# Gate and up tiles of a feed-forward phase interleaved on TensorE, with four slots of split weights

## The reference

```
x = x + mixed @ w_out                                   # 1024 -> 1024
h = rmsnorm(x, norm_ffn)
gate, ffn_new = causal_dwconv(h @ w_gate, ffn_past, ffn_conv_w, ffn_conv_b)   # width 3
x = x + (silu(gate) * (h @ w_up)) @ w_down              # 1024 -> 2816 -> 1024
```

## Time and profile before

| | us |
|---|---|
| three runs | 2597.19, 2600.63, 2600.97 |
| median | 2600.63 |
| the profiled execution | 2597.43 |
| its span in the trace | 2595.4 |

### The profile page before, as it was taken

The page is one execution under the profiler, slowest core; times in us unless marked ns, Lnnn a source line. Parts: engine busy times, 40 slices in busy tenths (PEclk is TensorE's granted clock), DMA queues, the critical chain, the costliest instruction groups (busy, mean ns, idle before and its releaser), DMA issues.

```text
span 2595.4 us, 33146 instructions
## 1 busy us (share of the span) xinstructions
PE 2368.6 (91%) x12571; PEld 2155.4 (83%) x12571; DVE 1057.6 (41%) x1983; ACT 999.4 (39%) x1676; POOL 1207.8 (47%) x629
## 2 busy tenths in 40 slices
PE   6999815977785799999999999999999999999998
PEld 6999814544443799999999999999999999999998
DVE  3687766059936433224332233231243231242212
ACT  4555311345552343344433334332333332343333
POOL 3544483025410455555455545444444444555554
PEclk9999958999996899999999999999999999999999
DMA  5544400200025454444543335433345333344443
GB/s 141 142 134 122 89 4 1 4 14 0 0 26 181 117 146 130 122 119 147 158 122 106 116 98 171 134 102 106 106 122 161 111 103 108 108 128 134 130 122 106
DMA packets 533462, 272.03 MB, mean 105 GB/s; under 512 B 95116, under 2 KB 527045, under 8 KB 533317
## 3 DMA queue, kind: packets, MB, share of 16 engines
q1 hardware_dynamic: 533317, 270.06, 36.7%
HBM read 252.65 MB, written 17.43 MB: 104 GB/s over the span
## 4 chain that ended last, share of the span: by engine, by line
PE 67%; DVE 1%; DMA 0%; SPq 0%; ACT 0%; issue 0%; ACTq 0%
PE ffn_bank L138 22%; PE ffn_bank L139 22%; PE ffn_bank L140 22%; PE ffn_bank L2323 1%; PE ffn_bank L2227 1%; DMA ffn_w_raw<-in_w_out 0%; DVE ffn_xm_lo L2060 0%; PE ffn_bank L2248 0%; SPq L1835 0%; DVE ffn_xT L2072 0%; DVE ffn_bank L2093 0%; DVE ffn_yrow L2143 0%; ACT ffn_xm_hi L1949 0%; SPq L1832 0%; SPq L1864 0%
## 5 line engine op out<-in xcount | busy, mean ns | idle before, releaser
L1928 POOL TENSOR_TENSOR ffn_w_lo<-ffn_w_raw,ffn_w_hi 128x1024 fp32r<-128x1024 f32 (+1 forms) x380 | 889.1, 2341 | 865.8 <-ACT ffn_w_hi L1937 865.6
L138 PE MATMUL ffn_bank<-ffn_xf_hi,ffn_w_hi 128*128 128x386 f32 (+5 forms) x1760 | 626.1, 356 | 5.7 <-DVE ffn_xf_lo L2124 5.7
L139 PE MATMUL ffn_bank<-ffn_xf_lo,ffn_w_hi 128*128 128x386 f32 (+5 forms) x1760 | 623.3, 354 | 0.0
L140 PE MATMUL ffn_bank<-ffn_xf_hi,ffn_w_lo 128*128 128x386 f32 (+5 forms) x1760 | 622.1, 353 | 0.0
L1937 ACT ACTIVATE ffn_w_hi<-ffn_w_raw 128x1024 fp32r<-128x1024 f32 (+1 forms) x380 | 391.5, 1033 | 579.4 <-PE ffn_bank L140 358.4
L138 PEld LDWEIGHTS ffn_bank<-ffn_xf_hi,ffn_w_hi 128*128 128x128 f32 x1760 | 331.9, 189 | 20.8 <-issue 6.3
L139 PEld LDWEIGHTS ffn_bank<-ffn_xf_lo,ffn_w_hi 128*128 128x128 f32 x1760 | 333.0, 189 | 12.3
L140 PEld LDWEIGHTS ffn_bank<-ffn_xf_hi,ffn_w_lo 128*128 128x128 f32 x1760 | 332.5, 189 | 12.1
L138 PE MATMUL ffn_bank<-ffn_h_hi,ffn_w_hi 128*128 128x384 f32 (+2 forms) x880 | 312.0, 355 | 3.6 <-DVE ffn_xT L2072 3.6
L140 PE MATMUL ffn_bank<-ffn_h_hi,ffn_w_lo 128*128 128x384 f32 (+2 forms) x880 | 310.1, 352 | 0.0
L139 PE MATMUL ffn_bank<-ffn_h_lo,ffn_w_hi 128*128 128x384 f32 (+2 forms) x880 | 309.7, 352 | 0.0
(11 more groups left out here) (350 smaller groups left out, 3178.7 us busy)
## 6 DMA issues: line engine op xcount, KB each, us to landing
ffn_w_raw<-in_w_gate SPq DMA_DIRECT2D x220, 256.0 KB, 3.3
ffn_w_raw<-in_w_up SPq DMA_DIRECT2D x220, 256.0 KB, 3.2
ffn_w_raw<-in_w_down SPq DMA_DIRECT2D x160, 256.0 KB, 3.1
pin_w_raw<-in_w_in SPq DMA_DIRECT2D x120, 256.0 KB, 3.4
ffn_w_raw<-in_w_out SPq DMA_DIRECT2D x160, 128.0 KB, 2.8
ffn_w_raw<-in_w_down SPq DMA_DIRECT2D x80, 192.0 KB, 2.6
mixed<-z_t SPq DMA_DIRECT2D x40, 208.0 KB, 2.2
pin_xrow<-in_x_prompt SPq DMA_DIRECT2D x15, 512.0 KB, 5.9
```

What stands on the lines that cost most here:

```text
L138: pe.matmul(out, w_hi, x_hi, start=first, stop=False)
L139: pe.matmul(out, w_hi, x_lo, start=False, stop=False)
L140: return pe.matmul(out, w_lo, x_hi, start=False, stop=last)
L1928: pool.tensor_tensor(w_lo[n % 3][:, 0:c], w_raw[n % 2][:, 0:c], w_hi[n % 3][:, 0:c].bitcast(F32), ALU.subtract).then_inc(s_lo, 1)
```

## The change

The gate and the up tile of a feature are computed together. For each of the eight slices, and each of the three passes, a matmul of the gate tile is followed by the matmul of the up tile with the same pass; they go to the two banks in turn. Both units must be split before the pair starts, so PE waits once, at the start of the pair, for `w_lo` of both, and for both of the things that a bank must be free of (`conv` for the gate bank, `h_lo` for the up bank). Both units are given back at the end of the pair. `w_hi` and `w_lo` get a fourth slot each, and ACT's `hi` runs four units ahead in place of three. The norm stages through two banks (2 and 3) in place of three, with `scaled_lo` of slice k-2 ahead of `scaled` of slice k on DVE. At the start of the phase the fourth `hi` is placed ahead of the fourth `mixed_hi`.

```diff
-        w_hi = [m.sb(f"w_hi{i}", [P, KD * P], F32R) for i in range(3)]
-        w_lo = [m.sb(f"w_lo{i}", [P, KD * P], F32R) for i in range(3)]
+        w_hi = [m.sb(f"w_hi{i}", [P, KD * P], F32R) for i in range(4)]
+        w_lo = [m.sb(f"w_lo{i}", [P, KD * P], F32R) for i in range(4)]
...
-        stage_b = bank[1:4]
+        stage_b = bank[2:4]
...
             def hi(n):
-                if n >= 3:
-                    act.wait_ge(s_used, n - 2)
+                if n >= 4:
+                    act.wait_ge(s_used, n - 3)
...
             def after(n):
 
-                if n + 3 < UNITS:
-                    hi(n + 3)
+                if n + 4 < UNITS:
+                    hi(n + 4)
...
-            for n in range(3):
+            for n in range(4):
                 hi(n)
                 mixed_hi(0, n)
-            mixed_hi(0, 3)
...
                     for k in hook.get(o, ()):
+                        if k >= 2:
+                            scaled_lo(b, k - 2)
                         scaled(b, k)
-                        if k:
-                            scaled_lo(b, k - 1)
                     if o == 5:
+                        scaled_lo(b, KD - 2)
                         scaled_lo(b, KD - 1)
...
             def gate_up(b, f):
-                fi, fw = b * NF + f, fwidth(b)
-                for s, (bk, c0) in enumerate(((gate_b[f % 2], 0), (up_b[f % 2], HALO))):
-                    n = n_gu(b, f, s)
-                    nb = HALO + fw - c0
-                    if fi >= 2:
-                        pe.wait_ge((s_conv, s_hlo)[s], fi - 1)
...
-                    pe.wait_ge(s_lo, n + 1)
-                    for k in range(KD):
...
-                        ins = three_passes(pe, bk[:, 0:nb], w_hi[n % 3][:, at], w_lo[n % 3][:, at],
-                                           xf_hi[:, k, c0:c0 + nb], xf_lo[:, k, c0:c0 + nb], k == 0, k == KD - 1)
-                    ins.then_inc(s_used, 1)
+                fi, fw, n = b * NF + f, fwidth(b), n_gu(b, f, 0)
+                if fi >= 2:
+                    pe.wait_ge(s_conv, fi - 1)
+                    pe.wait_ge(s_hlo, fi - 1)
...
+                pe.wait_ge(s_lo, n + 2)
+                both = ((gate_b[f % 2][:, 0:HALO + fw], n % 4, slice(0, HALO + fw)), (up_b[f % 2][:, 0:fw], (n + 1) % 4, slice(HALO, HALO + fw)))
+                for k in range(KD):
...
+                    for w_part, x_part, first, last in ((w_hi, xf_hi, k == 0, False), (w_hi, xf_lo, False, False), (w_lo, xf_hi, False, k == KD - 1)):
+                        for bk, slot, cols in both:
+                            ins = pe.matmul(bk, w_part[slot][:, at], x_part[:, k, cols], start=first, stop=last)
+                            if last:
+                                ins.then_inc(s_used, 1)
```

More of the change, by code:

```diff
@@ L1927, in _ @@
                 pool.wait_ge(s_hi, n + 1)
-                pool.tensor_tensor(w_lo[n % 3][:, 0:c], w_raw[n % 2][:, 0:c], w_hi[n % 3][:, 0:c].bitcast(F32), ALU.subtract).then_inc(s_lo, 1)
+                pool.tensor_tensor(w_lo[n % 4][:, 0:c], w_raw[n % 2][:, 0:c], w_hi[n % 4][:, 0:c].bitcast(F32), ALU.subtract).then_inc(s_lo, 1)
         @block.scalar
@@ L1974, in norm_hi @@
                 for of, to, n in halves(b):
-                    ins = act.activation(xf_hi[:, k, HALO + to:HALO + to + n], stage_b[i % 3][:, of:of + n], ACT.Copy)
+                    ins = act.activation(xf_hi[:, k, HALO + to:HALO + to + n], stage_b[i % 2][:, of:of + n], ACT.Copy)
                 ins.then_inc(s_xhi, 1)
@@ L2110, in scaled @@
                 dve.wait_ge(s_rstd, b + 1)
[L2111 to L2112 removed]
+                if i >= 2:
+                    dve.wait_ge(s_xlo, i - 1)
                 if k == 0 and b:
                     dve.wait_ge(s_hlo, b * NF)
[L2115 removed]
+                dve.scalar_tensor_tensor(out=stage_b[i % 2][:, 0:n], in0=xT[b % 2][:, k, 0:n], scalar=gain[:, k:k + 1], in1=turn_b[1][:, 0:n],
                                          op0=ALU.mult, op1=ALU.mult).then_inc(s_xn, 1)
@@ L2240, in make_out @@
                     at = slice(k * P, (k + 1) * P)
-                    ins = three_passes(pe, out_b[o % 2][:, 0:nb], w_hi[n % 3][:, at], w_lo[n % 3][:, at], xm_hi[:, k, 0:nb], xm_lo[:, k, 0:nb],
+                    ins = three_passes(pe, out_b[o % 2][:, 0:nb], w_hi[n % 4][:, at], w_lo[n % 4][:, at], xm_hi[:, k, 0:nb], xm_lo[:, k, 0:nb],
                                        k == 0, k == KD - 1)
@@ new lines, in gate_up @@
+                if fi >= 2:
+                    pe.wait_ge(s_conv, fi - 1)
+                    pe.wait_ge(s_hlo, fi - 1)
+                for g in range(1, 3):
+                    if f == first_tile(g):
+                        pe.wait_ge(s_y, (3 * b + g - 1) * KD + 6)
+                if f == 0 and b:
+                    pe.wait_ge(s_y, (3 * b - 1) * KD + 6)
+                pe.wait_ge(s_lo, n + 2)
+                both = ((gate_b[f % 2][:, 0:HALO + fw], n % 4, slice(0, HALO + fw)), (up_b[f % 2][:, 0:fw], (n + 1) % 4, slice(HALO, HALO + fw)))
@@ L2287, in down @@
                     at = slice(i * P, (i + 1) * P)
-                    ins = three_passes(pe, down_b[o % 3][:, 0:fw], w_hi[n % 3][:, at], w_lo[n % 3][:, at], h_hi[:, i, 0:fw], h_lo[:, i, 0:fw],
+                    ins = three_passes(pe, down_b[o % 3][:, 0:fw], w_hi[n % 4][:, at], w_lo[n % 4][:, at], h_hi[:, i, 0:fw], h_lo[:, i, 0:fw],
                                        i == 0, i == FG[g] - 1)
```

16 lines of the change are left out of this document (5 added, 11 removed).

## The result

The changed kernel takes 2614.72 us (median of 6, 2610.7 to 2616.74) against 2599.4 of the kernel before (2594.78 to 2600.97). The ratio is 1.006, with a 95% interval of 1.0047 to 1.0073: **15 us slower**, inside the forecast range and on the forecast side, with almost twice the loss of the forecast 8.3. It is more than the 5 to 13 us of the prediction's own rival A; the stated range was wider than that band. The profiled execution has a span of 2610.4 us against 2595.4.

What follows compares the result with a forecast made beforehand. TensorE was taken as the bound. Waits of 3.5 us in block 0 and 4.5 in block 1, plus 0.3 at the phase's start, gave +8.3 us: median 2609 us, range 2588 to 2622.

Steps and rivals of the forecast that it cites:

- rival A: Waits for weights around f = 7 and the first `down` tiles cost +5 to +13 us: 2606 to 2614; chance 0.42.
- What bounds it: Whole FFN phase: TensorE is the bound; only the distance between matmuls or new PE waits can change the time.
- the alternation is worth 0: Gate and up matmuls: switching banks leaves the distance unchanged, 0 for 5280 matmuls, bounds -84 to +11 us.
- Rival C: Gate and up matmuls: alternating banks shorten their distance; 2593 at 3 ns each, 2525 at 16 ns; chance 0.16.
- Steady pairs, 0: Steady gate and up pairs: results and weights come in time, 1.95 us to spare at 384 columns; cost 0.
- The loads behind DVE: Later `mixed_lo` holds SP's loads; PE waits at f = 7 and the first `down` group, blocks 0 and 1: 8.0 us.
- Blocks 2 and 3, 0: Waits behind the late `mixed_lo` in blocks 2 and 3: 0 to 0.9 us in block 2, counted as 0; block 3 the same.
- the second one goes faster than the first: Block 2: the second chain behind `mixed_lo` is quicker, its loads queueing with no row load; wait counted as 0.
- `mixed_lo` takes 2.2 us: DVE behind f = 4 in block 0: `mixed_lo` runs from 4.85 to 7.05 us behind the pair's end.
- The clock: PE's clock behind waits: waits of 0.9 us leave it at 1.00, so no cost was counted.
- rival D's milder form: Eight PE waits each drop the clock to 1.2 GHz for 18 matmuls: +21 us; chance 0.16, shared with stalling steady pairs.
- The fourth slot: Split weight buffers: makes the steady pair's cost zero; its own cost nothing, the number of `hi` and `w_lo` being unchanged.

Runs made afterwards that it cites:

- three-slot run: Changed kernel with three slots of split weights in place of four, ACT's `hi` three units ahead: 3193.88 us, ratio 1.2296.
- moving the loads: Changed kernel with the third and fourth `load_mix` moved in SP's queue from behind f = 6 and 7 to behind f = 8 and 9: 2596.64 us.
- moving the split: Changed kernel with `mixed_hi` and `mixed_lo` put in front of the chain of f = 4, 5, 8 and 9, SP's order kept: 2597.36 us.
- giving the lateness to the kernel before: Kernel before with the two critical `mixed_lo` of blocks 1 to 4 done four times each: 2632.07 us, ratio 1.0128.
- four-slot run: Kernel before with four slots of split weights and ACT's `hi` four units ahead, nothing else changed: 2606.42 us, ratio 1.0024.
- the kernel before with the loads moved: Kernel before with the third and fourth `load_mix` moved behind f = 8 and 9: 2599.9 us, ratio 0.9999.

## Why the prediction was right or wrong

- **What bounds it; the alternation is worth 0:** right. The one bank switch between the tiles told what 5280 of them would do: the pair is 8.46 against 8.48 us and 9.20 against 9.16. Rival C is out. The Trainium skill ("TensorE: Matmul & The Clock Gate", section "Back-to-back issue gap") gives columns/2.4 GHz plus 2.5 ns for isolated matmuls; an estimate by that formula is 0.163 us at 384 columns. The trace does not reach it: the pairs of 384 average 0.176 us in the changed kernel.
- **Steady pairs, 0:** right; no wait occurs in them, and the three-slot run bears the chain out, with a mean wait of 3.7 us and a longest of 4.4 where it gives 4.1.
- **The loads behind DVE:** the right mechanism at the right places, shown by moving the loads, by moving the split and by giving the lateness to the kernel before. The sizes, forecast against measured: block 0's pair 1.9 and 2.67, its `h_lo` 0.6 and 0.51; block 1's pair 2.4 and 2.53, its first `down` tile 1.8 and 2.44. Block 0's first `down` tile, forecast at 1.0, has none: the pair in front of it ran partly at 1.2 GHz, some 1.5 us longer, and used the time up. POOL has the piece at about 963.85 (961.45, plus the usual 2.40), and PE comes to it at 963.91.
- **Blocks 2 and 3, 0:** wrong, 1.94 us in block 2 (1.47 and 0.47) and 1.87 in block 3, all at the first `down` group. The step that failed is "the second one goes faster than the first". In block 2 of the kernel before it was 6.0 us from release to `hi` (1632.49 to 1638.47); now `hi` comes 7.2 us behind the release, from 1648.59 to 1655.79. In block 3 it is 6.3 and 7.9 us. The loads of block 2 on SP and the `hi` on ACT, before and then after:

```profile
1633.44 3.82 SPq L1848 DMA_DIRECT2D ffn_w_raw<-in_w_down  x4
1638.47 1.06 ACT L1937 ACTIVATE ffn_w_hi<-ffn_w_raw 128x1024 fp32r<-128x1024 f32 x1 [3.53 <-DMA ffn_w_raw<-in_w_down]
...
1649.55 2.32 SPq L1848 DMA_DIRECT2D ffn_w_raw<-in_w_down  x4
1655.79 1.06 ACT L1937 ACTIVATE ffn_w_hi<-ffn_w_raw 128x1024 fp32r<-128x1024 f32 x1 [7.38 <-DMA ffn_w_raw<-in_w_down]
```

  Now `mixed_lo` ends so late that both `w_raw` slots are free, and SP asks for two units (four DMAs) in 2.3 us in place of 3.8. That this is why the first of them lands later is likely, but no run tested it.
- **`mixed_lo` takes 2.2 us:** wrong, 2.68 and 2.93 in block 0. It got on only when POOL's `w_lo` was done, and the change put more of it beside that. It is about half of block 0's 2.67 against 1.9: the first `mixed_lo` ended 0.4 us later than forecast (7.4 behind the pair's end, not 7.05). The other half is the load: `hi` started 6.3 us behind SP's release and not 5.8.
- **The clock:** the forecast had it at 0, and only rival D's milder form had it, with 18 slow matmuls behind each of eight waits. Two waits of 2.4 to 2.7 us were followed by 10 and 9, about 3 us. The row I leaned on, waits of 0.9 us that leave the clock at 1.00, says nothing on waits three times as long, which my own sum contained.
- **The fourth slot, "its own cost is nothing":** wrong as a sentence, 6 to 9 us on the kernel before. The hand sum for f = 5 did use ACT's new order, so its price was in the sum, under the name of the pair's edges.

Sum of the misses: 3.8 us in blocks 2 and 3, 3.1 of clock less 1.3 in the first pair of block 0, 1.3 for the ends of the pipeline around the waits, 0.2 for the rest: 7.1, which takes 8.3 to 15.4. That the waits of blocks 0 and 1 come to 8.15 where 8.0 was forecast is partly luck, since single terms off by up to 1.0 cancel. Two small slips in the recorded working change nothing: the first `mixed_lo` of block 0 started 2.4 us behind the pair's end at 936.3, not 2.2, and rival D's 38 pairs of 384 columns without a load of `mixed` are 40 (18 in block 0, 22 in block 4).

The Trainium skill ("TensorE: Matmul & The Clock Gate", section "A second HAM failure mode: psum-queue depth-cycling") tells of a kernel that cycled through banks, idled briefly between its groups of matmuls, and saw its clock swing. Here the cycling alone did nothing of the kind: in the run with the loads moved the clock, at 1.2 GHz for the first 3.5 us of block 0 as it came from the wait in front, was at 1.00 for the rest of the 5280 matmuls. In the changed kernel it did fall, behind waits.

**Is there a version that beats both?** The changed kernel with the two loads moved is 18 us faster than the changed kernel; against the kernel before its ratio of 0.999 (0.9979 to 1.0001) is not clear of 1. The trace gives 1.3 us from block 0 on (1703.2 against 1704.5), and all of it lies in the first pair of block 0. From the first matmul of that pair to the first of the next, in the kernel before with the loads moved and then in the changed kernel with the loads moved:

```profile
893.87 0.66 PE L138 MATMUL ffn_bank<-ffn_xf_hi,ffn_w_hi 128*128 128x386 f32 x1 [5.73 <-DVE ffn_xf_lo L2124]
905.30 0.34 PE L138 MATMUL ffn_bank<-ffn_xf_hi,ffn_w_hi 128*128 128x386 f32 x1
...
895.07 0.66 PE L2268 MATMUL ffn_bank<-ffn_xf_hi,ffn_w_hi 128*128 128x386 f32 x1 [5.72 <-DVE ffn_xf_lo L2123]
905.16 0.34 PE L2268 MATMUL ffn_bank<-ffn_xf_hi,ffn_w_hi 128*128 128x386 f32 x1
```

That is 11.43 against 10.09 us, with the clock back at 1.00 some 3.4 us behind the first matmul in both. Tile by tile, PE takes a slice of `xf` for only three matmuls and has to wait for DVE's next one; in pairs it has six. (The kernel before needs 11.42 too, though its stretch at 1.2 GHz is 5.8 us long.) The prediction had put the first pair at 0. This 1.3 us is what the alternation is worth once its side effects are out of the way, by one trace of each; the medians can't tell it from 0.

## What to carry to other kernels

Before a release is moved later, list what each in-order queue has behind the operation that waits for it, and follow that through to the engine that is the bound: here 2.8 us on DVE became 12 us of waits on TensorE through SP's queue, and through ACT's, which ran a unit further ahead. A buffer more is not free on an in-order engine, since its reader moves up one place and takes other work's place in front of a wait. And look whether the old trace already has the new order somewhere: here one row, the step at the bank's change, told what 5280 of them would gain.

## What the runs showed of the hardware

**DVE's subtraction of two SBUF operands and POOL's do not run at the same time; the one that began first goes on.** In the changed kernel the first `mixed_lo` of block 0 ends at 941.43, 0.88 us behind POOL's end (935.77 + 4.78 = 940.55), the second at 954.54, 0.89 behind POOL's end (953.65), though they began at different distances from it; the three copies above did the same. It holds the other way round too. In the run with four copies one subtraction on DVE was under way when POOL began (DVE, then POOL):

```profile
942.92 1.03 DVE L2064 TENSOR_TENSOR ffn_xm_lo<-ffn_ms,ffn_xm_hi 128x832 fp32r<-128x832 f32 x1
943.35 2.86 POOL L1929 TENSOR_TENSOR ffn_w_lo<-ffn_w_raw,ffn_w_hi 128x1024 fp32r<-128x1024 f32 x1 [2.41 <-ACT ffn_w_hi L1938]
```

DVE took 1.03 us, as it does with POOL idle, and POOL 2.86 in place of its usual 2.40; the 2.79 of the row at 957.30 above is such a case as well. Work on PSUM operands went on: `h_lo` took its usual 0.56 us in the middle of POOL's operation.

```profile
950.82 0.56 DVE L2165 TENSOR_TENSOR ffn_h_lo<-ffn_bank,ffn_h_hi 128x384 fp32r<-128x384 f32 x1 [0.89 <-ACT ffn_h_hi L2017]
```

The Trainium skill ("GPSIMD Engine Reference", section "1. Specifications") says that the SBUF interfaces are shared with VectorE and names contention with DVE instructions that have two SBUF inputs; the traces agree, and show that for this pair of operations it is all or nothing, with a cost to whichever comes second.

**The clock** fell behind waits of 2.67 and 2.44 us and not behind 2.53, 1.87 and 1.47 us in one and the same run, for 10 and 9 matmuls. The length of the wait alone does not decide it: in the four-slot run ten slow matmuls follow a wait of 1.90 us. What tells these waits apart is open; no run here was made for it.
